# A two-layer decoder trunk on one core: memory attention, first feed-forward step and start-up in another order

## The reference

```python
for l in range(2):
    h = rms_norm(x, norm_mix[l])
    q, k, v = (h @ w_in[l]) split in 16 heads of 64      # three kinds of attention
    x = x + mix(q, k, v) @ w_out[l]
    # memory cross-attention: 4 heads of 64, 256 memory rows
    q = rms_norm(rms_norm(x, norm_cross[l]) @ w_mq[l], qn_mem[l])
    k, v = rms_norm(mem, norm_mem[l]) @ w_mkv[l]         # k is normed too
    p = softmax(q @ k.T * 64 ** -0.5)
    x = x + (p @ v) @ w_mo[l]
    # SwiGLU, inner width 2816
    g, u = rms_norm(x, norm_ffn[l]) @ w_gate_up[l]
    x = x + (silu(g) * u) @ w_down[l]
```

## Time and profile before

| | |
|---|---|
| median of 3 runs | 716.48 us (715.83, 716.48, 720.67) |
| the profiled execution | 719.07 us |
| its span, first to last instruction | 717.3 us |
| mean granted TensorE clock | 0.988 of full speed |
| busy share of the span: PE, DVE, ACT, POOL | 97%, 69%, 55%, 14% |

### The profile page before, as it was taken

One profiled execution on the slowest core, in us unless ns is written; L12 is line 12 of the kernel. 1 busy time (PEld: TensorE's weight loads), 2 busy tenths in 40 slices (PEclk: granted clock), 3 DMA queues, 4 the chain that ended last, 5 costly groups with the idle time before them and its releaser, 6 DMA issues.

```text
span 717.3 us, 10772 instructions
## 1 busy us (share of the span) xinstructions
PE 695.6 (97%) x3794; PEld 580.5 (81%) x3794; DVE 498.3 (69%) x988; ACT 394.6 (55%) x643; POOL 99.4 (14%) x92
## 2 busy tenths in 40 slices
PE   7999999989999999999999999999899999999997
PEld 6777787778888888888878877868688888888886
DVE  4898967573866666666668888675566666666665
ACT  5865866474744444444457567764755444444442
POOL 6331020217000000000021410302440000000000
PEclk9999999996999999999999999999999999999999
DMA  8845332245266666665554634312455566666631
GB/s 301 303 152 175 125 131 71 87 117 167 83 193 195 184 186 201 196 177 175 175 176 176 208 124 152 109 55 68 112 176 173 176 177 204 203 198 198 189 117 59
DMA packets 121216, 115.64 MB, mean 161 GB/s; under 512 B 3008, under 2 KB 95312, under 8 KB 121184
## 3 DMA queue, kind: packets, MB, share of 16 engines
q1 hardware_dynamic: 120080, 112.80, 50.7%
q0 software_dynamic: 384, 1.14, 0.5%
q10 hardware_dynamic: 720, 1.30, 0.5%
HBM read 114.17 MB, written 1.05 MB: 161 GB/s over the span
## 4 chain that ended last, share of the span: by engine, by line
PE 79%; DVE 10%; ACT 5%; issue 2%; POOL 2%; DMA 1%; ACTq 0%; DVEq 0%; POOLq 0%
PE ps L1872 20%; PE ps L1497 14%; PE ps L1877 11%; PE ps L1909 5%; PE ps L1910 5%; PE ps L1911 5%; PE ps L1566 3%; PE ps L1894 3%; DVE wlo L893 3%; PE ps L1840 2%; PE ps L1449 2%; ACT whi L594 2%; PE ps L1627 1%; PE ps L1423 1%; PE ps L1641 1%
## 5 line engine op out<-in xcount | busy, mean ns | idle before, releaser
L893 DVE TENSOR_TENSOR wlo<-raw,whi 128x2048 fp32r<-128x2048 f32 (+1 forms) x96 | 213.9, 2246 | 39.9 <-ACT whi L594 39.7
L594 ACT ACTIVATE whi<-raw 128x2048 fp32r<-128x2048 f32 (+1 forms) x103 | 190.9, 1878 | 14.0 <-PE ps L1911 7.3
L1872 PE MATMUL ps<-both,whi 128*128 128x512 f32 x640 | 159.2, 391 | 0.0
L1872 PEld LDWEIGHTS ps<-both,whi 128*128 128x128 f32 x640 | 117.6, 188 | 22.8
L1497 PE MATMUL ps<-whi,both 128*128 128x512 f32 x384 | 101.1, 399 | 3.3 <-ACT both L606 2.3
L841 ACT ACTIVATE qkv<-ps 128x512 f32<-128x512 f32 x44 | 26.4, 599 | 126.9 <-PE ps L1877 121.7
L1877 PEld LDWEIGHTS ps<-both,wlo 128*128 128x128 f32 x640 | 87.3, 190 | 6.2
L1877 PE MATMUL ps<-both,wlo 128*128 128x256 f32 x640 | 89.2, 282 | 0.0
L1497 PEld LDWEIGHTS ps<-whi,both 128*128 128x128 f32 x384 | 70.7, 189 | 19.5 <-issue 2.2
L1909 PE MATMUL ps<-whi,ahi 128*128 128x512 f32 x176 | 69.2, 393 | 1.6 <-DVE alo L1382 1.6
L1910 PE MATMUL ps<-wlo,ahi 128*128 128x512 f32 x176 | 69.0, 392 | 0.0
(11 more groups left out here) (210 smaller groups left out, 927.2 us busy)
## 6 DMA issues: line engine op xcount, KB each, us to landing
raw<-in_w_gate_up SPq DMA_DIRECT2D x88, 512.0 KB, 5.0
raw<-in_w_in SPq DMA_DIRECT2D x23, 1024.0 KB, 5.1
raw<-in_w_down SPq DMA_DIRECT2D x22, 1024.0 KB, 5.0
raw<-in_w_out SPq DMA_DIRECT2D x8, 1024.0 KB, 5.0
raw<-in_w_mkv SPq DMA_DIRECT2D x4, 1024.0 KB, 5.4
raw<-in_w_mq SPq DMA_DIRECT2D x4, 512.0 KB, 3.5
raw<-in_w_mo SPq DMA_DIRECT2D x2, 1024.0 KB, 4.8
raw<-in_w_in SPq DMA_DIRECT2D x4, 256.0 KB, 5.8
```

The source lines that it names most:

```text
L594: ins = act.activation(whi[s][:, cols], raw[s][:, cols], ACT.Copy)
L893: ins = dve.tensor_tensor(wlo[s][:, cols], raw[s][:, cols], hi, ALU.subtract)
L1872: pe.matmul(ps[:, bank, :], whi[s][:, a:a + P], both[:, :, k, :], start=(k == 0), stop=False)
```

## The change

It reorders and adds no arithmetic of the reference. Its parts:

1. Memory attention. Tile 0's query starts ahead of the last half of `out1_half(1, 1)`, whose parts stand between the query and its transposes. Tile 0's scores stand between tile 0's and tile 1's query. ScalarE makes tile 0's exponentials before it takes out tile 1's query. The squares of tile 1 move from ScalarE to VectorE. `split_hi` of `U_MO` moves behind `queryT_out(1)`. The output products that don't need `wlo` of `U_MO` come first (parts 0 and 2, tile 0), part 1 later. Three dummy products (`warm_up(3, ...)`) are added. PSUM banks and the place of the heads in `thi` and `tlo` (chunks 4 and 5) follow.
2. Parts of `products` (queries): low stream by high weights comes second, high stream by low weights third, in both layers.
3. Feed-forward. Quarters are built and split in the order 0, 2, 1, 3; `gate_up(0, 0)` starts with columns 0 to 3 (quarters 0 and 2) in parts 0 and 1, then columns 4 to 7; quarter 3 is built after the first of these steps.
4. Start. The DMA of tile 0 of x moves to SyncE's queue behind that of the identity, ahead of the weights. Two dummy products stand ahead of each of the products 1 to 3 of the first piece. The second unit's high part is made in four pieces with a signal each (`second_hi`).
5. Tables. `S_AT[8]` 83 to 81, `T_AT[3]` 69 to 67, `N_AT` up to 2 steps earlier for four entries, `HB_AT` 1 earlier, `CHAIN_AT[3]` 53 to 52, `MEM_AT` 1 later, `MEM_SQ_AT` 22 to 21, `KM_AT` 92 to 93, `MEM_ROOT_AT` 38 to 40.

```diff
@@ sync
             sp.dma_start(ident, consts["ident"]).then_inc(s_ident.sem, 16)
+            sp.dma_start(xs[:, 0, :], x_in[:, 0, :]).then_inc(s_x[0].sem, 16)
@@ scalar
-            act.dma_start(xs[:, 0, :], x_in[:, 0, :]).then_inc(s_x[0].sem, 16)
...
+                if layer == 0 and u == 1:
+                    for k in range(4):
+                        cols = slice(512 * k, 512 * k + 512)
+                        ins = act.activation(whi[s][:, cols], raw[s][:, cols], ACT.Copy)
+                        ins.then_inc((second_hi if k < 3 else hi_done[s]).sem, 1)
+                    return
...
                 squares_of_x(layer, 1, 0)
-                split_hi(layer, 20)
...
                 x_hi(layer, X_CROSS, 2)
                 query_out(0)
-                x_hi(layer, X_CROSS, 3)
                 queryT_out(0)
-                squares_of_x(layer, 1, 1)
+                x_hi(layer, X_CROSS, 3)
+                mem_exps(0)
+                mem_exps(1)
                 query_out(1)
+                act.wait_ge(m_pT_ps.sem, m_pT_ps.at(layer, 1))
+                act.activation(m_probT[0], ps[:, M_PT_BANKS[0], :], ACT.Copy).then_inc(m_pT_act.sem, 1)
                 queryT_out(1)
+                split_hi(layer, U_MO)
+                mem_exps(2)
+                mem_exps(3)
...
+                heads_of_memory_hi(0)
                 split_hi(layer, U_FFN)
                 split_hi(layer, U_FFN + 1)
+                heads_of_memory_hi(1)
+                for q in FFN_ORDER:
+                    x_hi(layer, X_FFN, q)
@@ vector
+                add_out(0, (0, 1))
+                for q in range(2):
+                    x_lo(layer, X_CROSS, q)
+                split_lo(layer, U_MQ)
+                add_out(1, (0,))
+                split_lo(layer, U_MQ + 1)
+                x_lo(layer, X_CROSS, 2)
+                ask_q(0)
+                add_out(1, (1,))
+                mem_max(0)
+                mem_max(1)
+                x_lo(layer, X_CROSS, 3)
+                take_q(0)
+                mem_shift(0)
+                mem_shift(1)
+                squares_of_second_tile()
+                ask_q(1)
                 mem_probT(1)
+                take_q(1)
+                mem_max(2)
+                mem_shift(2)
+                mem_max(3)
+                mem_shift(3)
                 mem_out(0)
                 mem_probT(2)
+                mem_lo(0)
                 mem_probT(3)
-                mem_lo(0)
                 mem_out(1)
                 mem_lo(1)
...
-                for q in range(4):
+                for q in FFN_ORDER:
                     x_lo(layer, X_FFN, q)
@@ tensor
-                parts = [(thi, whi), (thi, wlo), (tlo, whi)]
-                if layer == 0 and u < 2:
-                    parts = [(thi, whi), (tlo, whi), (thi, wlo)]
+                parts = [(thi, whi), (tlo, whi), (thi, wlo)]
...
                     for k in range(4):
+                        if first_piece and k:
+                            warm_up(2)
...
+                for part in range(3):
+                    out1_half(1, 1, part, 0)
+                query(0, 0)
+                build_x(layer, X_CROSS, 2)
+                query(0, 1)
+                for part in range(2):
+                    out1_half(1, 1, part, 1)
+                pe.wait_ge(mq_out.sem, mq_out.at(layer, 1))
+                transpose_pair(qm, 0, MEM_T_BANKS[0], 0, qmT_ps)
+                out1_half(1, 1, 2, 1)
+                pe.wait_ge(kmT_out.sem, kmT_out.at(layer, 1))
+                mem_score(0)
+                build_x(layer, X_CROSS, 3)
+                for h in range(2):
+                    query(1, h)
+                mem_transpose_p(0)
+                mem_transpose_p(1)
+                pe.wait_ge(mq_out.sem, mq_out.at(layer, 2))
+                transpose_pair(qm, 1, MEM_T_BANKS[1], 0, qmT_ps)
+                mem_weigh_v(0)
+                mem_score(1)
+                mem_weigh_v(1)
+                warm_up(3, M_PT_BANKS[0])
+                mem_transpose_p(2)
+                pe.wait_ge(om_ready.sem, om_ready.at(layer, 1))
+                transpose_pair(om, 0, MEM_T_BANKS[0], SEQ, omT_ps)
+                mem_transpose_p(3)
+                output(0, (0, 1), (0, 2))
+                mem_weigh_v(2)
+                mem_weigh_v(3)
+                output(0, (0,), (1,))
                 pe.wait_ge(om_ready.sem, om_ready.at(layer, 2))
-                transpose_pair(om, 1, 7, SEQ, omT_ps)
+                transpose_pair(om, 1, MEM_T_BANKS[1], SEQ, omT_ps)
+                output(0, (1,), (1,))
+                output(1, (0,), (0, 1, 2))
+                build_x(layer, X_FFN, 0)
+                output(1, (1,), (0,))
                 build_x(layer, X_FFN, 2)
+                build_x(layer, X_FFN, 1)
+                output(1, (1,), (1, 2))
...
+                    halves = (range(0, 4), range(4, KC))
+                    steps = ((0, halves[0]), (1, halves[0]), (0, halves[1]), (1, halves[1]), (2, range(KC)))
+                    for part, chunks in steps if b == 0 else ((part, range(KC)) for part in range(3)):
+                        if part == 0 and b == 0:
+                            pe.wait_ge(t_hi.sem, t_hi.at(layer, 4 * X_FFN + 2 + 2 * (chunks[0] > 0)))
...
+                        if b == part == 0 and chunks[0] == 0:
+                            build_x(layer, X_FFN, 3)
```

More of the change, by code:

```diff
@@ L967, in per_head, with add_to_x @@
                 return r.unsqueeze(3).to_broadcast((P, T, heads, HD))
-            def add_to_x(layer, stage, t, bank, scale=None):
-                for c in range(2):
+            def add_to_x(layer, stage, t, bank, scale=None, columns=(0, 1)):
+                for c in columns:
                     if (stage, t, c) in SUMS:
@@ L1266, in _, with add_out, squares_of_second_tile @@
                 heads_lo(3)
[L1267 to L1273, removed]
+                def add_out(t, columns):
+                    add_to_x(layer, 0, t, lambda t, c: OUT1_BANKS[t][c], columns=columns)
+                def squares_of_second_tile():
+                    dve.wait_ge(x_new.sem, x_new.at(layer, 4))
+                    dve.tensor_tensor_reduce(sq[:, D:2 * D], xs[:, 1, :], xs[:, 1, :], 1.0, 0.0, ALU.mult, ALU.add, ss[:, 1:2])\
+                       .then_inc(ss_done.sem, 1)
                 def ask_q(t):
@@ L1480, in piece @@
                     first_piece = layer == u == t == part == 0
-                    if part == 0 and not first_piece:
+                    second = layer == t == part == 0 and u == 1
+                    if part == 0 and not first_piece and not second:
                         pe.wait_ge(hi_done[s].sem, hi_done[s].at(layer, fill(u) + 1))
@@ L1494, in piece @@
                             pe.wait_ge(first_hi.sem, 1)
-                        elif first_piece:
+                        elif second and k < 3:
+                            pe.wait_ge(second_hi.sem, k + 1)
+                        elif first_piece or second:
                             pe.wait_ge(hi_done[s].sem, 1)
@@ L1741, in _ @@
                     out1_half(0, 1, part, 1)
-                for half in range(2):
-                    for part in range(3):
-                        out1_half(1, 1, part, half)
                 def transpose_pair(src, t, bank, col, sig):
@@ L1839, in output @@
                                 a = k * D + 512 * c
-                                ins = pe.matmul(mo_acc(t, c), x_part[:, k, tok], w_part[s][:, a:a + 512],
-                                                start=part == k == 0, stop=part == 2 and k == 1)
-                        if 2 not in parts:
+                                ins = pe.matmul(mo_acc(t, c), x_part[:, 4 + k, tok], w_part[s][:, a:a + 512],
+                                                start=part == k == 0, stop=part == final and k == 1)
+                        if final not in parts:
                             continue
@@ L1936 @@
 QK_CHUNKS = (0, 1, 2, 3)
-CHAIN_AT = (14, 26, 46, 53)
+CHAIN_AT = (14, 26, 46, 52)
 QKT_AT = (30, 43, 56, 72)
-S_AT = (45, 47, 55, 61, 67, 70, 73, 78, 83, 86)
-T_AT = (54, 57, 64, 69, 71, 72, 76, 77, 78, 79, 83, 84, 88, 91, 92, 93)
+S_AT = (45, 47, 55, 61, 67, 70, 73, 78, 81, 86)
+T_AT = (54, 57, 64, 67, 71, 72, 76, 77, 78, 79, 83, 84, 88, 91, 92, 93)
 V_AT = (64, 67, 67, 71, 77, 77, 78, 79, 82, 82, 88, 88, 92, 92, 98, 98)
@@ L1946 @@
 SUB_AT = 73
-MEM_AT = (18, 19, 20, 21)
-MEM_SQ_AT = 22
-HB_AT = (81, 83, 92)
-KM_AT = 92
+MEM_AT = (19, 20, 21, 22)
+MEM_SQ_AT = 21
+HB_AT = (80, 82, 91)
+KM_AT = 93
 N_BUILD = 2
-N_AT = (76, 77, 81, 82, 85, 86, 89, 90)
+N_AT = (76, 77, 80, 81, 83, 84, 89, 90)
 LAM_AT = 13
-MEM_ROOT_AT = 38
+MEM_ROOT_AT = 40
 LAST = max(FILLERS + 3 * len(OUT1_EARLY) - 1, V_AT[-1])
@@ L1962 @@
 OUT0_BANKS = (7, 5, 6, 7)
+QM_BANKS = (4, 6)
+MEM_T_BANKS = (5, 7)
+M_PT_BANKS = (4, 0, 4, 6)
 OUT1_BANKS = ((5, 4), (6, 7))
```

137 lines of the change are left out of this document (46 added, 91 removed).

## The result

The changed kernel takes 711.98 us (median of 11 runs, 710.96 to 714.23); the kernel before, run beside it on the same chip, 716.48 (11 runs, 714.94 to 721.33). The ratio is 0.9922, with a 95% interval of 0.99 to 0.9945. The profiled execution of the changed kernel took 711.93 us, its span 710.1, and its mean granted clock is 1.0, against 0.988 in the profiled execution before.

A forecast was written before the change was run, and what follows sets the result against it. TensorE, busy for 97% of the span, was taken as the bound, through its waits, clock and added products. Terms -2.3 - 1.4 - 0.2 = -3.9 us took the median from 716.48 to 712.6; range 707.5 to 717.5.

The forecast's parts named there:

- Memory attention and first feed-forward step: Query of tile 0 to diagonal product: new order gives -1.1 us a layer, -2.3 in both (-4.5 to +1).
- the third rival: Memory attention: the waits only move, 0 gained there, total 714.9 us; chance 0.2.
- End of the attention: Wait for the probability copy falls to about 0.2 through `S_AT[8]` at 81: -0.7 us a layer, -1.4 in both.
- The other tables give nothing: End of the attention: tables other than `S_AT[8]` gain nothing; `KM_AT` costs some 0.5 us if its cover is gone.
- Start: First 44 us, not bound by TensorE: `freqs` one place further ahead in ScalarE's queue gives -0.2 us (0 to -0.45).
- the rival with a chance of 0.2: Memory attention: the clock stays up in both layers, -3.9 - 5.0 us, total 707.6; chance 0.2.
- The second rival: Memory attention: the clock falls in both layers, one more low stretch costs +5.0 us, total 717.6; chance 0.15.
- the gap that I feared: Memory attention, layer 1, 514.9 to 517.5: only two blocks of transposes, a pair of them and waits, besides the first.
- The prediction's bound for it: Memory attention: a clock falling in both layers was to be decided from 3.9 us of low clock on.

The follow-up runs named there:

- the repetition: The changed kernel, unchanged, run again beside the kernel before: 712.04 us (12 runs), ratio 0.9931.

## Why the prediction was right in its number and not in its sum

712.6 was forecast and 711.98 measured. That the two agree is luck: the forecast was -3.9 us of order at an unchanged clock, and the measured -4.5 is 2.1 of order and the rest mostly clock. Neither of the two theories of the experiments holds whole: the order is worth 2.1 us, and more than half of the gain is the clock.

**Memory attention and first feed-forward step: -2.3 forecast, -0.9 measured** (0.46 + 0.44 at an equal clock). This is the term that was mis-sized (its 1.12 a layer make 2.2, written as 2.3). The steps came in the order forecast, with most waits where I had put them. The query starts where the last three parts of `out1_half(1, 1)` started before, at 499.19; 6.84 us added to the changed kernel's times bring both to that point, and my marks and the rows then compare so:

| layer 1 | forecast | measured + 6.84 |
|---|---|---|
| query | 499.2 | 499.19 |
| tile 0's scores | 504.2 | 504.37 |
| first transposes | 509.9 | 510.08 |
| tile 1's scores | 512.6 | 512.97 |
| third block | 516.0 | 516.38 |
| first part 1 | 521.1 | 521.51 |
| `gate_up(0, 0)` | 526.9 | 527.65 |
| diagonal | 533.8 | 534.59 |

All marks are late, and by more and more: 0.2, 0.4, 0.8. The prediction gave each mark 0.2 and let them chain; it didn't expect errors of one sign. It started each step the moment its releaser ended, while the rows show 0.11 us from the end of quarter 3's high part to its low part and 0.05 from the end of that to TensorE's product. That this makes up the 0.8 isn't shown, and the 0.3 that come up between the first part 1 and `gate_up(0, 0)` lie where the timeline lists no wait of TensorE. Of 1.1 us expected against the 534.92 of the earlier trace rows, 0.33 stayed (0.44 if both are counted from the copy product). The first transposes are 2.0 earlier (2.2 forecast), the query waits 0.43 (0.7), the third block 0.52 (about 1), `split_lo` on GpSimd starts at 509.13, takes 13.67 / 3 = 4.6 and so ends 1.0 ahead of the first part 1 at 514.67, as forecast. The squares on VectorE take 1.22 at 501.93 and are covered: VectorE then still waits 1.24 for the query copy.

I credited the gain to the wrong part. The fillers between the queries only move the waits, as the third rival said; the run with the feed-forward in the old order shows all of the gain in the order of quarters and of the first feed-forward step. What holds the new order of memory attention back is a point of my own list, the shifts on VectorE behind the low part of quarter 3: moved ahead of it (with the old order of parts), 1.2 us a layer come out.

**End of the attention: -1.4 forecast, -1.2 measured** (0.59 + 0.64). Size right, cause wrong. "The other tables give nothing" failed: `S_AT[8]` alone gave 0.1, all tables 0.6 a layer. I had asked what the earlier pair of scores takes off the chain to the probability copy, and not what it pushes back, ScalarE's copies of heads. Which of the other tables does it wasn't tried.

**Start: -0.2 forecast, unresolved.** The wait for `mlo` was passed anywhere between 42.24 and 46.21 us in the profiled executions of all variants, and at 43.91 and 45.71 in two of one program. A gain of 0.2 can't be seen in that. That the start isn't TensorE's fits: taking its dummies out changed nothing. The wait there grew from 0.58 to 1.67, as said. The step that the term rests on, that `freqs` is what counts, doesn't hold in the changed kernel's profiled execution. GpSimd's cast starts at 7.01 instead of 7.65, released by the positions, and VectorE's copy of the root comes at 22.85 instead of 23.72. But the low part of weights behind that copy starts at 24.11, against 23.80 before, because it waits 1.10 for ScalarE's high part, which had waited 1.55 for the DMA of the weights. In all thirteen profiled executions that wait for `mlo`, the wait is passed 19.8 to 20.4 us behind the start of that low part. Its releaser changes from one execution to the next: the root in some, the weights in others.

**Clock: the rival with a chance of 0.2 came true in part.** The clock stayed up in both layers; its price, 8.9 us off to 707.6, was too high, since the order gave 2.1 and not 3.9 and the median execution before holds less of the low clock than the profiled one. The median of before holds some low clock, the changed kernel hardly any (0.998 to 1.0 in all 23 executions). Execution by execution: 7.14 = 2.1 of order + 5.0 of clock. For the medians: 2.1 is order, and 2.8 is what separates the span of 716.0 (before, 33 runs) from 713.2, the middle of the five executions of before with a clock of 0.997 or more. Together they make 4.9, between the 4.5 of the result and the 5.6 of the repetition (717.62 against 712.04). What is left over either way I can't place; it is within what the start moves. The second rival, a clock that falls in both layers, did not occur: the gap that I feared is 0.5 us long with the dummies and 1.24 without. The prediction's bound for it, 3.9 us of low clock, is the time that it costs and not its length: a stretch of 13.65 us at the lower level cost 5.0. Both the order and the dummies help: each alone gives clocks between those of before and after. What decides in one execution whether the clock falls isn't shown; the same program did both.

## What to carry to other kernels

Where TensorE is busy for 97% of the time, a gap of a microsecond is worth more than its length if a low stretch can follow it: repeat the kernel before until its clocks are seen on both sides, and compare orders between the same two instructions at the same clock. A few dummy products in such a gap cost nothing there (52.60 with them, 52.53 without) and were worth 2.8 us to the kernel before. When a step is moved up, ask on each engine what it pushes back, and when a new order gives nothing, look for the small operation that stands ahead of its chain (here one low part ahead of the shifts, 1.2 us a layer).

## What the runs showed of the hardware that was not expected

- At the wait for `mlo`, near 44 us, a wait of 2.89 us was followed by 3.41 us at the lower clock, and so was one of 1.92 in the run with the old order of parts; the shorter waits at that place, 0.53 to 1.72 in eleven executions, weren't.
- A low stretch is not always of one length: in memory attention the profiled executions had 3.41 (dummies in the kernel before), 6.83 and 10.24 (all tables) and 13.65 us (the kernel before, and the scores two steps earlier). The one of 13.65 in layer 0 of before was still on while TensorE was busy for 5.00 of 5 us.
- Two executions of one program pass the same wait up to 1.8 us apart (43.91 and 45.71), and spans at a clock of 0.999 or more differ by up to 3.8 us, more than the whole gain of the order. The later one has its first weights 0.8 us later (VectorE starts on their second piece at 10.50 instead of 9.67) and 3.41 us of low clock from 12 us on; whether these make up the 1.8 isn't shown.
